# Zeros written in long runs, weight copies limited to three under way, kept columns in small tiles, and gated norm and pooling in fewer VectorE steps, in a two-layer decoder on eight cores

## What is computed

```python
for l in range(DEPTH):                      # 2
    m = hybrid_mixer(x, ...)
    x = layer_norm(ALPHA * x + m, ln1_g[l], ln1_b[l])
    f = grouped_moe(x, router_w, router_b, exp_w_gate[l], exp_w_up[l], exp_w_down[l])
    x = layer_norm(ALPHA * x + f, ln2_g[l], ln2_b[l])

def hybrid_mixer(x, ...):
    z = x @ w_in                            # 1024 -> 2048 columns, split among four groups
    y = concatenate([
        u * (w_s (lower triangle) @ layer_norm(v) + b_s),        # gated, chunks of 128 tokens
        silu(layer_norm(conv31(a * sigmoid(g)))) @ pw,           # conformer, 31 taps back
        (mean over the last 2, 4, 8 or 16 tokens - z) @ w_grp * scale,   # pooling, 64 channels each
        b_gate * conv3(c_gate * h)])                             # short conv, 3 taps back
    return group_rms_norm(y, mix_norm_g) @ w_o

def grouped_moe(x, ...):                    # 16 experts in 4 groups; best group per token, top 2 in it
    y = sum over experts e of gate[e] * ((silu(x @ w_gate[e]) * (x @ w_up[e])) @ w_down[e])
```

## Time and profile before

| | us |
|---|---|
| profiled execution | 1710.9 |
| span of its slowest core (4) | 1709.8 |
| spans of the other seven | 1632.4 to 1699.3 |
| PE, DVE, ACT, POOL busy, core 4 | 1275.7, 1004.8, 683.3, 189.4 |
| mixer stage of layer 0 (to the first expert load) | about 557 |
| expert stage of layer 0 | about 358 |
| mixer stage of layer 1 | about 415 |
| expert stage of layer 1 | about 380 |

### The profile page before, as it was taken

How to read it: one execution, slowest core, us unless ns; L and a number is a source line. 1 busy time by engine, 2 the same in 40 slices (tenths; PEclk the granted TensorE clock), 3 DMA queues, 4 the chain that set the end, 5 groups by cost and what they waited for, 6 DMA issues and landing times.

```text
span 1709.8 us, 26111 instructions; the slowest of 8 cores (1632.4 to 1709.8 us)
## 1 busy us (share of the span) xinstructions
PE 1275.7 (75%) x7610; PEld 682.6 (40%) x7610; DVE 1004.8 (59%) x2547; ACT 683.3 (40%) x1438; POOL 189.4 (11%) x324
## 2 busy tenths in 40 slices
PE   3887139787773796979773987889874697869795
PEld 2433013333452453445442433343443354445452
DVE  1666035756575374657581585776776365664767
ACT  3544024534452432333326453554643433442342
POOL 3001010010101011021113001010101011110111
PEclk8897659899896798989895999999996798979997
DMA  9898979686432598988987555648534598957681
GB/s 186 181 204 147 126 128 141 99 143 104 100 118 105 186 185 219 235 232 194 188 167 222 125 99 133 125 97 140 87 124 136 181 171 232 249 125 171 170 190 50
DMA packets 49224, 265.59 MB, mean 155 GB/s; under 512 B 9232, under 2 KB 9872, under 8 KB 33168
## 3 DMA queue, kind: packets, MB, share of 16 engines
q0 software_dynamic: 23984, 147.84, 48.4%
q1 hardware_dynamic: 25056, 115.53, 22.3%
HBM read 327.08 MB, written 109.18 MB: 255 GB/s over the span
## 4 chain that ended last, share of the span: by engine, by line
PE 53%; DMA 13%; DVE 11%; issue 11%; ACT 7%; another core or an unknown queue 4%; SPq 0%; DVEq 0%; ACTq 0%; POOL 0%; POOLq 0%
PE ps L622 34%; PE ps L1617 15%; DMA s_x<-xs_rows 5%; DVE s_x L664 3%; PE ps L625 3%; ACT s_f L638 3%; DMA x_rows<-s_x,s_toki 2%; DMA s_f<-gmwT 2%; DMA s_x<-x 2%; ACT s_b L638 1%; DMA s_x<-x_rows 1%; DVE s_r L651 1%; DVE s_sm L681 1%; DMA out<-s_x,s_toki 1%
## 5 line engine op out<-in xcount | busy, mean ns | idle before, releaser
L1617 PE MATMUL ps<-s_k 128*128 128x384 bf16 x2048 | 356.8, 334 | 11.6 <-DVE s_k L672 7.0
L622 PE MATMUL ps<-s_k,s_y 128*128 128x512 bf16 x1296 | 318.4, 396 | 32.3 <-DVE s_y L651 15.0
L622 PE MATMUL ps<-s_k 128*128 128x512 bf16 (+2 forms) x1400 | 281.4, 355 | 76.2 <-DVE s_gcnt L651 58.9
L1617 PEld LDWEIGHTS ps<-s_k 128*128 128x128 bf16 x2048 | 203.0, 100 | 151.5 <-issue 25.7
L625 PE MATMUL ps<-s_identb,s_b 128*128 128x128 bf16 x920 | 91.2, 258 | 168.8 <-ACT s_b L638 86.9
L622 PEld LDWEIGHTS ps<-s_k,s_y 128*128 128x128 bf16 x1296 | 127.2, 101 | 208.4 <-issue 90.2
L664 DVE SCALAR_TENSOR_TENSOR s_x<-s_x,s_sm,s_lp 128x1024 f32<-128x1024 f32 x162 | 203.7, 1276 | 10.1 <-ACT s_sm L638 7.3
L622 PEld LDWEIGHTS ps<-s_k 128*128 128x128 bf16 x1400 | 128.9, 105 | 195.5 <-issue 112.8
L638 ACT ACTIVATE s_f<-ps 128x384 f32<-128x384 f32 (+2 forms) x185 | 88.0, 487 | 266.3 <-PE ps L1617 215.3
L664 DVE SCALAR_TENSOR_TENSOR s_x<-ps,s_x 128x512 f32<-128x512 f32 x192 | 134.6, 743 | 42.4 <-PE ps L622 41.2
L625 PEld LDWEIGHTS ps<-s_identb,s_b 128*128 128x128 bf16 x920 | 79.2, 153 | 193.7 <-issue 189.3
(11 more groups left out here) (163 smaller groups left out, 1231.6 us busy)
## 6 DMA issues: line engine op xcount, KB each, us to landing
s_k<-bw SPq DMA_DIRECT2D x48, 1024.0 KB, 7.9
s_x<-xs_rows SPq DMA_DIRECT2D x48, 514.0 KB, 10.8
bw<-exp_w_gate POOLq DMA_DIRECT2D x16, 1024.0 KB, 12.8
bw<-exp_w_up POOLq DMA_DIRECT2D x16, 1024.0 KB, 16.0
bw<-exp_w_down POOLq DMA_DIRECT2D x16, 1024.0 KB, 14.4
s_k<-exp_w_gate POOLq DMA_DIRECT2D x16, 1024.0 KB, 13.2
s_k<-exp_w_up POOLq DMA_DIRECT2D x16, 1024.0 KB, 13.4
s_k<-exp_w_down POOLq DMA_DIRECT2D x16, 1024.0 KB, 11.6
```

The source lines that it names most:

```text
L622: pg.add(PE, lambda e: e.matmul(out.ap, lhsT.ap, rhs.ap, start=start, stop=stop), [out], [lhsT, rhs], d)
L1617: pg.add(PE, lambda en, o=o, lt=lt, rv=rv, kc=kc: en.matmul(o.v(lambda ap: ap.rearrange("p (s t) -> p s t", t=128)).ap, lt.ap, rv.ap, star ...
```

## The change

1. `zero_rows` fills a whole `k` tile (4096 bf16, read as 2048 f32) and writes xs_rows as one flat array in 14 DMAs of 128 x 2048 f32 and one of 128 x 1140: 8192 bytes in a run for each partition. It is called in block 0, and waits for the second load of w_o. The router of block 0 is no longer held back.
2. `copy_ahead` also waits until the third copy before it has landed. A load from bw may stand in the program only once four more copies stand behind its own, as long as copies are left to do.
3. The columns kept for the next block are copied by GpSimd to small tiles (new pool `ch`, and `sm`, which goes from 12 tiles to 10, so the `h` and `f` tiles come free when their own block is done).
4. `G_tile`: the norm's subtract and scale, the product with ln_g and the addition of ln_b (three steps) become subtract with product, and scale with addition (two).
5. `P_section`: the two half-height steps (64 partitions each) become one of full height, after a ScalarE copy of 64 partitions that brings both windows into one tile; the same for the fix of the first 16 tokens.

The core of the diff:

```diff
         def zero_rows(deps):
-            zt = Tile(XO)
+            zt = newk()
             mset(DVE, zt(), 0.0)
-            dma(SP, x1_d[0:HALO, :], zt(0, D), [ZD(31, 32)], [zt(0, D)], 128 * D * 4, deps=deps)
-            for q in range(NQ + 5):
-                dma(SP, xs_d[q * 128:(q + 1) * 128, :], zt(), [ZD(q, q + 1)], [zt()], 128 * XW * 4, deps=deps)
+            z = zt().v(lambda ap: ap.bitcast(F32))
+            dma(SP, x1_d[0:HALO, :], z.v(lambda ap: ap[:, 0:D]), [ZD(31, 32)], [zt()], 128 * D * 4, deps=deps)
+            flat = xs_d.rearrange("r c -> (r c)")
+            n, q = (NQ + 5) * 128 * XW // 128, 0
+            while n:
+                m = min(n, 2048)
+                at = (NQ + 5) * 128 * XW - n * 128
+                dma(SP, flat[at:at + 128 * m].rearrange("(p n) -> p n", p=128), z.v(lambda ap, m=m: ap[:, 0:m]),
+                    [ZD(q, q + 1)], [zt()], 128 * m * 4, deps=deps)
+                n -= m
+                q += 1
...
+        def landed(k):
+            return k is None or k in (copied[:-4] if ahead else copied)
...
-            while stream and stream[0] is not None and inuse[0] < most and (stream[0][0] is None or stream[0][0] in copied):
+            while stream and stream[0] is not None and inuse[0] < most and landed(stream[0][0]):
...
         def copy_ahead(l, e, k):
-            deps = pg.ops[-1:]
+            deps = pg.ops[-1:] + made[-3:-2]
...
-            ts(DVE, vn(), puv(256, 512), s(6, 7), ALU.subtract, s(8, 9), ALU.mult)
+            stt(vn(), puv(256, 512), s(6, 7), lw.bc3(0, 256), ALU.subtract, ALU.mult)
             vb = Tile(GB)
-            tt(DVE, vn(), vn(), lw.bc3(0, 256), ALU.mult)
-            tt(DVE, vb(), vn(), lw.bc3(256, 512), ALU.add)
+            stt(vb(), vn(), s(8, 9), lw.bc3(256, 512), ALU.mult, ALU.add)
...
-                    cpy(ACT, h(0, 30), st_.h[j](st_.nb, st_.nb + 30))
+                    cpy(ACT, h(0, 30), st_.h(j * 32, j * 32 + 30))
...
-            st_.h = hs
+            st_.h = Tile(CHP)
+            for j in range(2):
+                cpy(POOL, st_.h(j * 32, j * 32 + 30), hs[j](nb, nb + 30))
...
-                for (p0, p1) in ((0, 64), (64, 128)):
-                    s = X if p0 == 0 else Y
-                    stt(pl(0, nb, p0, p1), s(15, 15 + nb, p0, p1), invw(j, p0, p1), z(15, 15 + nb, p0, p1), ALU.mult, ALU.subtract)
...
+                cpy(ACT, Y(15, 15 + nb, 0, 64), X(15, 15 + nb, 0, 64))
+                stt(pl(0, nb), Y(15, 15 + nb), invw(j, 0, 128), z(15, 15 + nb), ALU.mult, ALU.subtract)
...
-                    if l == 0 and b == 1:
-                        zero_rows(pg.ops[-1:])
+                    if l == 0 and b == 0:
+                        zero_rows([lw.wo[1].load])
                         zeroed.append(pg.ops[-1])
-                        cnt, gcn = router(0, 0, *held, cnt, gcn)
```

More of the change, by code:

```diff
@@ L715, in build @@
         inuse = [0]
-        copied = set()
+        copied = []
+        made = []
         def newk():
```

35 lines of the change are left out of this document (20 added, 15 removed).

## The result

The changed kernel takes 1637.9 us (median of four runs, 1633.5 to 1648.1); beside it the kernel before took 1729.7 (four runs). The ratio is 0.950, with a 95% interval of 0.943 to 0.957. The forecast was 1696 us and a range of 1662 to 1728, so the gain was 92 us where I had forecast 34, and the time lies under the range.

What follows compares the result with a forecast made beforehand. The kernel was taken as held mostly by matmuls and short chains between them, plus one hole in layer 0. Gains of 29 us (hole) and 5 us (mixer) from the 1730.2 median gave 1696 us, range 1662 to 1728.

Steps and rivals of the forecast that it cites:

- The zeros' start: Mixer of layer 0: zeros flow from 76 us, after x loads through at about 73 and 3 us for the memset.
- The zeros' length: Mixer of layer 0: filling xs_rows takes 60 us (263 GB/s), between 38.5 and 81, ending at 136.
- Rival A: Zeros in layer 0 don't get faster, 195 GB/s whatever the run; gain 13 us, time 1717; chance 0.25.
- rival B: Zeros in layer 0 go near the bw loads' rate, end at 115 to 120; gain 45 to 51; 1675; chance 0.27.
- From the zeros to the cast: Layer 0: six weight copies instead of seven before ScalarE's cast of the awaited x tile, 69.5 us instead of 79.2.
- ScalarE's wait of some 35 us: Sign in layer 0's mixer: ScalarE still waits some 35 us for x before its cast, instead of 63.1.
- The hole: Layer 0's mixer, TensorE mostly idle from 155 to 235 us, ScalarE waiting for x: 29 us gained, cast at 205.5.
- Rival D: x loads of later blocks starve behind copies; ScalarE's other waits, 14.5 us, double; time 1711; chance 0.08.
- The mixer, VectorE: Mixers: fewer gated norm and pooling steps save 27 us of VectorE, 5 us on the path; bounds 0 and 14.
- The kept columns: Mixers: 72 GpSimd copies of 2 to 30 columns, two h and four f tiles free a block earlier; costed at nothing.
- The limit on copies: Layer 0: each copy waits until the third before has landed; six instead of seven go ahead, 9.7 us per copy.
- The sum: Whole kernel: 1710.9 - 29 - 5 = 1676.9 us profiled; from the median, 1730.2 - 34 = 1696.

Runs made afterwards that it cites:

- h2_old_steps: Changed kernel with the gated norm's three old steps and the pooling's two half-height steps back: 0.988 of the kernel before (0.981 to 0.995).
- g1_kept_act: Kernel before with only the kept columns moved to small tiles, copied by ScalarE instead of GpSimd: mixer of layer 1 mean 409.4 us, no ratio.
- e2_kept: Kernel before with only the kept columns moved to small tiles by GpSimd: 0.992 of the kernel before (0.987 to 0.997).
- e4_limit: Kernel before with only the limit of three copies under way and later bw loads: 1.017 of the kernel before (1.010 to 1.024).
- e runs: Follow-up runs made on one chip; there the unedited changed kernel took 0.962 of the kernel before (0.949 to 0.975).
- f1_before: Kernel before, unedited, run again on another chip: 1.016 of itself (1.002 to 1.029), two executions.

## Why the prediction was wrong, point by point

**The zeros' start.** Forecast 76 us, of which 3 were for the memset. The memset took 3.47 us (3.7 forecast) and did not stand in the way: it ran at 48.58, and the zeros were issued from 70.99. But the four x loads ahead of them were issued at 67.55, not at 63.21, and those still flowed to about 78. So the zeros began some 2 us later than forecast, for another reason than I had given.

```profile
48.58 3.47 DVE L676 MEMSET s_k<- 128x4096 bf16 x1 [0.80 <-PE ps L623]
```

**The zeros' length.** This is the first step that failed. I took 60 us, the middle of 38.5 and 81, since "the row nearest in kind (writes by all cores) is the slow one, the row nearest in packet size the fast one". Measured: 350 GB/s, so 15.8 MB in 45 us, from about 78 to 123, and the scatter at 127 instead of 136. In the forecast's own count, from the start to the scatter, that is 49 us instead of 60. The bounds held it and the point between them was too cautious. The size of the packet wasn't what told the rows apart either: 4096 is as good as 8192. That 4112 is a multiple of 16 and of no larger power of two, so that every second row starts off any larger one, could be read from the row of 1028 f32, and I didn't ask about it. Rival A fell, rival B (an end at 115 to 120) was nearer than the forecast; its 45 to 51 us of gain were not reached, since the scatter came at 127.

**From the zeros to the cast.** Forecast 69.5 us; measured 195.8 - 127.2 = 68.6. Six copies, the fourth let go 17 us after the first, the x load landing as the sixth does: right, and so were the bw load ahead of it and its worth of nothing. ScalarE's wait of some 35 us was 33.8. The hole gained 38.8 us instead of 29: 8.8 of the excess is the scatter at 127.2 instead of 136, 0.9 the way from there to the cast.

**Rival D.** It came true beside the forecast: the x loads of later blocks starve. Without the hole, ScalarE's waits for x were 77.6 - 63.1 = 14.5 us and are 65.3 - 33.8 = 31.5. I had priced the doubling at 14.5 and given it 0.08; they grew by 17. The rest of layer 0's mixer became 6 us shorter all the same. That the gain of the kept columns covered these waits is my reading, no run shows it.

**The mixer, VectorE.** 5 us in all were forecast. With the rest in place 3 to 5 came out in layer 1 (h2_old_steps), which is within the spread of unedited runs: the term is neither confirmed nor refuted. The gated norm's two steps take 481 and 479 ns as forecast, and a copy of half height 614 in front of the pooling.

```profile
L665 DVE SCALAR_TENSOR_TENSOR s_g<-ps,s_sm,s_bc 128x256 f32<-128x256 f32 x33 | 15.9, 481 | 1.7
...
L671 ACT COPY s_f<-s_f 64x512 f32<-64x512 f32 x12 | 7.4, 614 | 3.5 <-DVE s_f L652 2.5 <-DVE s_sm L685 1.0
```

But in layer 0 the whole plan hangs on such steps: 37 to 44 us more without them.

**The kept columns.** This is the second step that failed, and the greater. "I cost this at nothing": I noted that "two h and four f tiles come free a block earlier" and then asked only whether the GpSimd copies would be late. They are not: ScalarE waits 13.8 us for them in the whole run (7.7 for those of f tiles, 6.1 for those of h tiles). Moving them is worth 26 us in layer 1, of which the tiles that they free have at least 14 (g1_kept_act). In layer 0 it may be some 7 to 11 us on core 4 (550.3 in e2_kept, 557.6 and 561.6 in the two profiles of before), but no comparison on one chip shows that. The trace had the bound that I should have used: in layer 1 TensorE is idle for 92 of 422 us, while ScalarE waits there only 5.6 us for x, and in such a stage a pool that is short is as good a candidate as an engine. The bound of 14 us above for the mixer was therefore no bound.

**The limit on copies.** Costed at nothing beyond the six copies. The six copies came by it, as e4_limit shows, and they are worth 10 us of the hole as forecast; the whole time shows nothing of the limit.

**The sum.** 38.8 + 6.1 - 1.7 + 26.3 + 2.4 = 72 us of the profiled execution. Of the 38 us that were missing, 10 are the hole's and 21 the mixer's in layer 1 beyond the 5 forecast; 4 lie in the rest of layer 0 and 2 in the experts of layer 1. The median gained 20 us more than the profile, since the kernel before's profiled execution was 19 us under its median. On the e runs' chip the changed kernel gained 65 us of 1703, by which the first median of before would have become some 1664, just inside the range. So that the time lies under the range rests in part on which executions were taken; that the two terms were too small does not.

## What to carry to other kernels

When an edit lets a tile of a pool go earlier, cost the tile, not only the copy that does it: where the busiest engine is idle for a fifth of a stage and no transfer explains it, the number of free tiles may be what holds it, and the idle time says how much there is to gain (here 16 of the 26 us were idle time, and 10 came with the higher granted clock). When a kernel writes DRAM in long runs that lie end to end, try to make their length a large power of two: 8192 bytes gained nothing over 4096 here, and lengths of 4112 and 8176, with starts at multiples of 16 only, cost a third to two thirds of the rate. And where a planner writes the order, parts don't add up (the zeros, the kept columns and the VectorE steps each alone gave 1.0%, 0.8% and nothing, the limit alone cost 1.7%, and all together gave 3.8%), so a part's worth is best found by taking it out of the whole as well as by adding it alone.

## What the runs showed of the hardware that I had not expected

- Eight cores that each write zeros from SBUF to DRAM, core 4 from 80 to 118 us: 340 to 351 GB/s in runs of 4096 or 8192 bytes that begin at multiples of their length, 204 to 232 with rows of 4112, 121 with runs of 8176.
- DRAM to DRAM copies with a cast, 2 MB read and 1 MB written: 9.7 to 9.9 us each where runs are whole, 15 us each with the halves in turn; x loads of 512 KB beside them took up to 67 us (42 for the one that ends the hole) and up to 14.6. Here the faster copies are the ones beside which the other queue waits longer.
- The mixer of layer 1 ran at a granted clock of 0.92 with fewer gaps and at 0.88 with more, and the same matmuls were busy for 318.7 and 329.1 us (e2_kept and f1_before). Which of the two brings the other isn't shown.
